# The end of a gated recurrence reordered, its states chained in place, and late weight tiles moved into its levels

## The chip, the cores and the metric

The kernel runs on one core of a Trainium2 chip. The metric is device time of one execution in microseconds (us); the table below gives the median of three runs. One more execution was profiled, and every row in this document that is marked as a profile comes from such a profiled execution.

## What is computed

Two layers of a diffusion backbone over 1024 latent tokens and 256 context tokens, model width 1024. Each layer mixes tokens with three groups of heads that read one input projection (A: neighbourhood attention, B: grouped attention with rotary positions, C: a gated recurrence that runs in both directions), joins them in one output projection, and then runs a gated convolutional feed-forward. Both halves are modulated by vectors computed from `c` and `c_ctx`, and each ends in a layer norm. What matters here:

```python
def gla_chunkwise(q, k, v, logf, s0):            # group C, chunks of 64 tokens
    def step(S, inp):
        qc, kc, vc, gc = inp
        b = jnp.cumsum(gc, axis=-2)
        ...
        att = jnp.einsum('bhtk,bhsk,bhtsk->bhts', qc, kc, decay)
        o = jnp.einsum('bhts,bhsv->bhtv', att, vc) + jnp.einsum('bhtk,bhkv->bhtv', qc * jnp.exp(b), S)
        b_last = b[..., -1:, :]
        S = S * jnp.exp(b_last[..., 0, :])[..., None] + jnp.einsum('bhsk,bhsv->bhkv', kc * jnp.exp(b_last - b), vc)
        return S, o

def hgrn2_readout(o, g, gn_g):
    y = rms_norm(o, gn_g) * jax.nn.silu(g)

# in each layer
mod = jnp.split((s_c @ w_ada[l] + b_ada[l])[:, None, :], N_MOD, axis=-1)     # w_ada[l]: 1024 x 6144
y = jnp.concatenate([o_a, o_b, o_c], axis=-1) @ w_out
x = layer_norm(DEEPNORM_ALPHA * x + mod[2] * y, ln1_g[l], ln1_b[l])
f = conv_ffn(modulate(x, mod[3], mod[4]), ...)                               # modulate(x) = layer_norm(x) * (1 + scale) + shift
```

The second layer gives out latent tokens only, so its projections run over 1024 columns where the first layer's run over 1280.

## The kernel before

The program of each engine is written out by hand; nothing is scheduled by a tool, and the order of a row in the source is the order on its engine. Engines wait for each other by semaphores. Activations lie by channel (128 channels x up to 1280 tokens, eight such tiles for width 1024). Every large product is made of three products of rounded halves: a weight tile is loaded (SyncE), split by GpSimd into a high and a low part (`split_tile`, L820 and on), an activation tile is split into `h_hi` (ScalarE, a copy) and `h_lo` (VectorE, a subtraction), and TensorE adds high by high, high by low and low by high (`gemm`, L1012). PSUM is used as two slots of three banks that take turns: a product may begin when the use before last of the slot has been read out ("freed"). `Plan` numbers these uses.

**Phase C, the recurrence.** Ten projections come first (forget gates f and b, input i, query q, gate g, each in two tiles of 128 channels, thus two heads each). Then the decay inside chunks of 64 is worked out by six levels (blocks of 1, 2, 4 ... 32): at each level and for each of the two tiles VectorE multiplies keys and queries in `c_x` by decays in `c_tot` (`longer`, L2075), ScalarE gathers keys into `c_ko`, TensorE makes the products within chunks (`att`, L1342 and L1346) and VectorE copies those that the level decides into `c_att` by a mask (`masked`, L2083). Behind the levels TensorE turns the keys (`turn_keys`, L872), ScalarE copies them to `c_kd`, TensorE makes what each chunk adds to its state (`added`, L1375) and ScalarE copies that to `c_d` (`take_added`). GpSimd spreads each chunk's whole decay over 64 values into `c_by` (`decays_by_value`, L840), and VectorE runs the states of all 20 chunks through one scan for each of four cases (two tiles, two directions; L2110) into `c_state`, which lies with the chunk as its last index, so that the 64 values of one chunk's state are 20 elements apart. `outputs` then adds for each tile the products with the own chunk (L1396) and with the incoming states (L1417), ScalarE takes the sum and its squares to `c_o`, TensorE averages the squares (`mean_squares`, L1428), ScalarE makes the reciprocal root and VectorE the gate (`gate`, L2125 and L2127).

**Late modulation tiles.** Of the modulation weights `w_ada`, 24 tiles of 1024 x 256 (1 MB) are not needed before a layer's end (16 in the second layer). In layer 0 eight of them are used during the projections; the other 16, and all 16 of layer 1, go through three slots of `ada_late`, which lie over the weight buffers that are idle during the levels. SyncE loads them (`load_late`), the first three when the last projection is done and each later one when the tile three before it has been used. TensorE uses them between the levels' products (`late`, L1038). Their sum is folded behind the outputs (L1048) and becomes `mods`.

**Phase O** is the output projection, whose first tile takes the eight activation tiles in `O_ORDER` as they become ready (0 to 2 from group A, 3 to 5 from B, 6 and 7 from C). ScalarE makes the first four high halves behind tile 0's reciprocal root (`end_of_recurrence`), VectorE the low halves behind tile 0's gate.

**Norm tails.** The layer norm behind phase O and behind the first feed-forward is not applied to the activations but folded into the next product by low rank rows. `norm_tail` runs three times: VectorE copies raw sums from PSUM to `sraw` (L1844), TensorE turns them so that tokens lie on partitions, VectorE works out mean and reciprocal deviation in some twenty steps on 12 values (`al`), writes three values per token into `colmat` in three parts (two alike, one negated), TensorE spreads first the reciprocal deviation and then `colmat` over a slot, and ScalarE and VectorE turn the latter into `rank_rows`: a rounded copy, and then the difference from it in the rows that `low_rows` marks (L1907). `correct` (L893) multiplies these rows.

## Time and profile before

| | us |
|---|---|
| median of three runs | 3658.02 |
| lowest and highest | 3657.78, 3658.77 |
| the profiled execution | 3653.44 |
| its span, first to last instruction | 3651.6 |
| TensorE products busy | 3436.2 (94%) |
| VectorE busy | 1634.5 (45%) |
| ScalarE busy | 1002.5 (27%) |
| GpSimd busy | 1077.7 (30%) |
| mean granted clock of TensorE | 0.979 |

Busy shares are means over phases that have different limits. Products overlap in the array, so a busy TensorE is not one at its peak. In the page and in the answers PE is TensorE, DVE is VectorE, ACT is ScalarE, POOL is GpSimd, SP is SyncE.

### The profile page before, as it was taken

What the parts mean: (1) busy time and instruction counts of PE and PEld (TensorE: products, weight loads), DVE (VectorE), ACT (ScalarE), POOL (GpSimd) and SP (SyncE); (2) the same over time, 40 slices, a digit from 0 to 9 for tenths busy, and PEclk for the clock granted to TensorE, in tenths of its full rate; (3) what the DMA queues carried; (4) which work ended last, traced back from release to release, by engine and by line L of the source; (5) the groups of instructions that cost most, each with busy time, mean ns of one, the idle gap of its engine ahead of it and who ended that gap; (6) DMA issues with size and microseconds to landing.
All of it is one profiled execution on the core that took longest, in us unless ns stands there. A gap on an engine that the chain in (4) does not pass through costs nothing.

```text
span 3651.6 us, 57048 instructions
## 1 busy us (share of the span) xinstructions
PE 3436.2 (94%) x24613; PEld 2836.9 (78%) x24613; DVE 1634.5 (45%) x2492; ACT 1002.5 (27%) x1435; POOL 1077.7 (30%) x408
## 2 busy tenths in 40 slices
PE   6999999979989999999999899999979899999998
PEld 5777778868868888888887677788867678888887
DVE  4333563065176334333434632463085563434436
ACT  4334564124122111111111333464133221111111
POOL 1212101304223333333332112201324244444443
PEclk9999999999989999999999899999989899999999
DMA  5111002252201111111112111001062111111111
GB/s 181 37 28 30 1 2 61 85 180 52 77 18 41 35 41 35 35 41 35 41 35 76 22 24 27 24 2 30 24 198 76 48 45 49 50 46 47 52 47 64
DMA packets 269677, 186.41 MB, mean 51 GB/s; under 512 B 45404, under 2 KB 249076, under 8 KB 269428
## 3 DMA queue, kind: packets, MB, share of 16 engines
q1 hardware_dynamic: 268272, 182.28, 16.7%
q8 instruction: 197, 3.23, 0.4%
q10 hardware_dynamic: 1156, 0.48, 0.1%
q14 instruction: 52, 0.43, 0.0%
HBM read 174.33 MB, written 8.39 MB: 50 GB/s over the span
## 4 chain that ended last, share of the span: by engine, by line
PE 84%; DVE 9%; issue 3%; ACT 2%; DMA 1%; POOL 1%; ACTq 0%; POOLq 0%; DVEq 0%; PEldq 0%
PE psum L1012 60%; PE psum L872 6%; PE psum L1112 5%; PE psum L881 3%; PE psum L1262 3%; PE psum L1190 2%; DVE f_t L2244 1%; DVE y_chan L2134 1%; DMA ada_late<-in_w_ada_dram 1%; PE psum L1417 1%; PE psum L941 1%; DVE c_x L2075 1%; PE psum L1221 1%; PE psum L1038 1%; ACT f_t L2774 1%
## 5 line engine op out<-in xcount | busy, mean ns | idle before, releaser
L1012 PE MATMUL psum<-h_hi,w_split 128*128 128x512 f32 (+1 forms) x5952 | 1438.0, 370 | 18.3 <-POOL w_split L834 8.1
L832 POOL TENSOR_SCALAR w_split<-w_raw 128x1024 fp32r<-128x1024 f32 x196 | 554.6, 2830 | 2308.3 <-PE psum L1012 1623.1
L1012 PEld LDWEIGHTS psum<-h_hi,w_split 128*128 128x128 f32 x5952 | 1030.7, 188 | 223.4 <-issue 12.1
L1012 PE MATMUL psum<-h_lo,w_split 128*128 128x512 f32 (+1 forms) x2976 | 800.1, 368 | 0.0
L1012 PEld LDWEIGHTS psum<-h_lo,w_split 128*128 128x128 f32 x2976 | 516.0, 188 | 97.6
L2244 DVE SCALAR_TENSOR_TENSOR f_t<-psum,vec,f_t 128x1023 f32<-128x1023 f32 (+1 forms) x264 | 260.2, 1013 | 704.5 <-ACT f_t L2774 701.3
L834 POOL TENSOR_TENSOR w_split<-w_raw,w_split 128x1024 fp32r<-128x1024 f32 x196 | 476.9, 2433 | 16.3
L1012 PE MATMUL psum<-f_hi,w_split 128*128 128x512 f32 (+1 forms) x1696 | 417.2, 371 | 15.7 <-DVE y_chan L2134 10.7
L2774 ACT ACTIVATE f_t<-psum,vec 128x1280 f32<-128x1280 f32 (+1 forms) x88 | 115.4, 1311 | 909.4 <-PE psum L1012 887.1
L1012 PEld LDWEIGHTS psum<-f_hi,w_split 128*128 128x128 f32 x1696 | 295.9, 188 | 80.4 <-issue 25.4
L2134 DVE SCALAR_TENSOR_TENSOR y_chan<-psum,mods,y_chan 128x1024 f32<-128x1024 f32 (+1 forms) x256 | 247.1, 1002 | 172.2 <-PE psum L1012 171.9
L1012 PE MATMUL psum<-f_lo,w_split 128*128 128x512 f32 (+1 forms) x848 | 233.8, 370 | 0.0
L1012 PEld LDWEIGHTS psum<-f_lo,w_split 128*128 128x128 f32 x848 | 149.3, 188 | 28.3
L872 PE MATMUL psum<-ident,o_chan 128*128 128x128 f32 x1016 | 151.6, 282 | 6.6 <-ACT a_pt L2348 3.1
L2436 ACT ACTIVATE o_chan<-o_chan,stats 128x1280 f32<-128x1280 f32 (+3 forms) x153 | 152.7, 998 | 0.0
L2348 ACT ACTIVATE b_pt<-psum 128x512 f32<-128x512 f32 (+1 forms) x204 | 113.5, 581 | 110.5 <-PE psum L872 110.5
L872 PEld LDWEIGHTS psum<-ident,o_chan 128*128 128x128 f32 x1016 | 108.2, 141 | 36.6 <-issue 28.2
L2050 DVE TENSOR_SCALAR c_tot<-c_x 128x2560 f32<-128x2560 f32 x4 | 6.0, 1490 | 288.4 <-PE psum L1012 288.4
L1112 PE MATMUL psum<-b_pt,b_v 128*64 128x128 f32 x1968 | 130.9, 278 | 0.4 <-DVE b_pt L1739 0.4
L1112 PEld LDWEIGHTS psum<-b_pt,b_v 128*64 128x64 f32 x1968 | 105.4, 137 | 18.1 <-issue 17.3
L1726 DVE CUSTOM_DVE_ANT_1 o_chan<-psum,zeros 128x1280 f32<-128x1280 f32 (+1 forms) x81 | 100.1, 1264 | 34.9 <-PE psum L1262 33.9
L2348 ACT ACTIVATE f_hi<-f_t 128x1280 fp32r<-128x1280 f32 (+1 forms) x44 | 51.4, 1168 | 194.0 <-DVE f_t L2257 194.0
(276 smaller groups left out, 3502.6 us busy)
## 6 DMA issues: line engine op xcount, KB each, us to landing
w_raw<-in_w_up_dram SPq DMA_DIRECT2D x88, 512.0 KB, 3.8
ada_late<-in_w_ada_dram SPq DMA_DIRECT2D x32, 1024.0 KB, 6.9
w_raw<-in_w_down_dram SPq DMA_DIRECT2D x44, 512.0 KB, 3.8
w_raw<-in_w_in_dram SPq DMA_DIRECT2D x42, 512.0 KB, 3.9
ada<-in_w_ada_dram SPq DMA_DIRECT2D x4, 2048.0 KB, 18.0
ada_early<-in_w_ada_dram SPq DMA_DIRECT2D x8, 1024.0 KB, 5.2
x_first<-in_x_dram SPq DMA_DIRECT2D x8, 512.0 KB, 12.7
o_x<-in_x_dram SPq DMA_DIRECT2D x8, 512.0 KB, 3.9
```

Source lines behind the costliest of these rows:

```text
L832: pool.tensor_scalar(w_hi[:, n % 2], w_raw[:, n % 2], 1.0, None, ALU.mult).then_inc(s["w_hi_done"], 1)
L834: pool.tensor_tensor(w_lo[:, n % 2], w_raw[:, n % 2], w_hi[:, n % 2].bitcast(F32), ALU.subtract)\
L872: return pe.transpose(out_ap, in_ap, ident[0:rows_, 0:rows_])
L881: last = pe.matmul(acc[:, t0:t0 + tn], weight, a[:, k, t0:t0 + tn], start=(k == 0 and j == 0), stop=(k == KT - 1 and j == 2))
L1012: last = pe.matmul(columns(key, t0, t0 + tn), weight, a[:, k, t0:t0 + tn], start=(k == order[0] and j == 0), stop=(k == order[-1] and j == 2))
L1112: last = pe.matmul(psum[rows_, OUT_BANK, 0:P], values(b)[:, rows_], turned_to(unit, head)[:, P * b:P * b + P], start=(k == 0), stop=(k == ...
L1262: ins = pe.matmul(scores_at(unit, hh)[:, t0:t0 + tn], q_[rows_], k_[rows_, t0:t0 + tn], start=pass_ == 0, stop=pass_ == 2)
L2134: ins = dve.scalar_tensor_tensor(out=y_chan[:, m, a:b], in0=columns(key, a, b), scalar=mods[:, l, KT * mod + m, who:who + 1], in1=base[:, ...
L2244: ins = dve.scalar_tensor_tensor(out=dst, in0=src, scalar=vec[:, at_col:at_col + 1], in1=dst, op0=ALU.mult, op1=ALU.add)
L2348: return act.activation(dst, src, ACT.Copy, scale=scale)
L2436: say(f"probs_ready{head}", act.activation(p, p, ACT.Exp, scale=-1.0, bias=stats[:, 0, c_:c_ + 1], accum_out=stats[:, 2, c_:c_ + 1]))
L2774: say("conv_start", act.activation(f_t[:, half, 0:w], slot(*key)[:, 0:w], ACT.Identity, scale=vec[:, mid:mid + 1], bias=vec[:, shift:shift ...
```

## The change

1. `c_state`, `c_by` and `c_d` go. ScalarE copies what chunks add straight into `c_x`, where the turned keys no longer are needed, chunk by chunk with 64 values side by side, and VectorE runs each state in place: 18 steps, for both directions in turn, each `state = state_before * decay + added` with the decay as a scalar per channel. `decays_by_value` on GpSimd goes.
2. `outputs` waits for the states behind the products with the own chunk, no longer ahead of them.
3. `O_ORDER` becomes 2, 3, 4, 5, 0, 1, 6, 7. The first four high halves stand ahead of ScalarE's `take_outputs(0)`, the first two low halves ahead of VectorE's new `mods`; `c_o` is moved so that they have room. Inside `outputs(1)` mean squares come behind four chunk pairs (two before) and the folding behind six (four before).
4. Late tiles: two are used behind level 0's products and none behind level 6's, where before it was none and three. The slots start from 0 in each layer, and the first three loads wait each for their own buffer only: the first for the last projection but one, the second for the last weight tile's split, the third for the last projection.
5. Norm tail: ScalarE copies the upper half of `sraw`. `colmat` is written by token as rounded values and their differences from the exact ones, so that `rank_rows` is one copy by ScalarE.

The diff, cut to its core:

```diff
-O_ORDER = [0, 1, 4, 5, 2, 3, 6, 7]
+O_ORDER = [2, 3, 4, 5, 0, 1, 6, 7]
...
-                sp.wait_ge(*full("C", l, C_PARTS[-1][0]))
+                first_free = [full("C", l, C_PARTS[-2][0]), (s["w_ready"], plan.tile["in", l, C_PARTS[-1][1]] + 1),
+                              full("C", l, C_PARTS[-1][0])]
                 for j in range(N_EARLY[l], len(late_tiles(l))):
+                    if j - N_EARLY[l] < 3:
+
+                        sp.wait_ge(*first_free[j - N_EARLY[l]])
                     load_late(j)
...
                 for n in range(len(STEPS) + 1):
                     for tile in range(2):
                         att(n, tile)
-                        if n:
-                            late(2 if n >= 3 and tile else 1)
+                        if n == 0:
+                            late(2 * tile)
+                        elif n < len(STEPS):
+                            late(2 if n > 1 and tile else 1)
...
-                for k, (tile, way) in enumerate(WAYS):
-                    dve.wait_ge(s["by_ready"], 4 * l + k + 1)
-                    dve.wait_ge(s["d_ready"], 4 * l + k + 1)
-                    say("state_ready", dve.tensor_tensor_scan(
-                        c_state[:, k].rearrange("p v i -> p (v i)"), c_by[:, k].rearrange("p v i -> p (v i)"),
-                        c_d[:, k % 2].rearrange("p v i -> p (v i)"), 0.0, ALU.mult, ALU.add))
+                for tile in range(2):
+                    passed = [None, None]
+                    for i in range(1, NCH - 1):
+                        for way in range(2):
+                            k = 2 * tile + way
+                            if i == 1:
+                                dve.wait_ge(s["d_ready"], 4 * l + k + 1)
+                            else:
+                                dve.wait_ge(*passed[way])
+                            ins = dve.scalar_tensor_tensor(out=state_of(k, i), in0=state_of(k, i - 1),
+                                                           scalar=c_el[:, tile, way, i:i + 1], in1=state_of(k, i),
+                                                           op0=ALU.mult, op1=ALU.add)
...
                 dve.wait_ge(s["late_used"], n_late(l))
                 take_modulation_rows(2 if l < DEPTH - 1 else 1)
+                for k in O_ORDER[0:2]:
+                    low_half(l, k)
                 dve.wait_ge(s["mods_full"], l + 2)
...
-                for p in (0, 2):
-                    w = P * groups_[p][1]
-                    last = also(dve.tensor_copy(sraw[32 * p:32 * p + 64, 0:w], psum[32 * p:32 * p + 64, 7, 0:w]))
+                say("sraw_ready", dve.tensor_copy(sraw[0:64, 0:P * groups_[0][1]], psum[0:64, 7, 0:P * groups_[0][1]]))
...
+                for part in (0, 4):
+                    also(dve.tensor_copy(to(part), four(high.bitcast(F32))))
+                last = also(dve.tensor_tensor(to(8), four(whole), four(high.bitcast(F32)), ALU.subtract))
...
-                dve.wait_ge(s["rank_hi"], st + 1)
-                dve.wait_ge(*release(dve.scalar_tensor_tensor(
-                    out=rank_rows[:, 0:w], in0=slot(*key)[:, 0:w], scalar=low_rows[:, 1:2], in1=rank_rows[:, 0:w].bitcast(F32),
-                    op0=ALU.mult, op1=ALU.add), *key))
```

How the order of instructions moves, at three places. In the lists `xN` counts equal instructions, and the brackets name the semaphores waited for. Line numbers behind the change are those of the changed kernel.

TensorE in layer 0, from the last of level 0's products to those of level 1 (`c_x 64x64` is level 0, `c_x,c_ko` level 1, `ada_late,cond` a late tile). Before:

```order
L1342 MATMUL psum<-c_x 64x64 [waits shared_bank]
L1342 MATMUL psum<-c_x 64x64 x7
L1346 MATMUL psum<-c_x,c_ko 64x64 [waits freed0,ko_ready,x_ready]
L1346 MATMUL psum<-c_x,c_ko 64x64 x35
L1346 MATMUL psum<-c_x,c_ko 64x64 [waits shared_bank]
L1346 MATMUL psum<-c_x,c_ko 64x64 x3
L1038 MATMUL psum<-ada_late,cond 32x128 [waits late_landed0]
L1038 MATMUL psum<-ada_late,cond 32x128 x15
```

And now:

```order
L1345 MATMUL psum<-c_x 64x64 [waits shared_bank]
L1345 MATMUL psum<-c_x 64x64 x7
L1041 MATMUL psum<-ada_late,cond 32x128 [waits late_landed0]
L1041 MATMUL psum<-ada_late,cond 32x128 x15
L1041 MATMUL psum<-ada_late,cond 32x128 [waits late_landed1]
L1041 MATMUL psum<-ada_late,cond 32x128 x15
L1349 MATMUL psum<-c_x,c_ko 64x64 [waits freed0,ko_ready,x_ready]
L1349 MATMUL psum<-c_x,c_ko 64x64 x35
L1349 MATMUL psum<-c_x,c_ko 64x64 [waits shared_bank]
L1349 MATMUL psum<-c_x,c_ko 64x64 x3
L1041 MATMUL psum<-ada_late,cond 32x128 [waits late_landed2]
```

Two late tiles have moved ahead of level 1's first products.

VectorE in layer 0, from the whole decays (`c_el`) to the gate of tile 0. Before:

```order
L2105 COPY c_el<-c_tot 128x2x19
L2110 SCALAR_TENSOR_TENSOR c_state<-c_by,c_d 128x1280 [waits dve_step,d_ready,by_ready]
L2110 SCALAR_TENSOR_TENSOR c_state<-c_by,c_d 128x1280 [waits d_ready,by_ready] x3
L1656 COPY mod_rows<-psum 128x256 [waits late_used]
L1661 TENSOR_TENSOR mods<-psum,vec 128x64 [waits dve_step,mods_full]
L1667 TENSOR_SCALAR mods<-mods 128x16 [waits dve_step]
L1661 TENSOR_TENSOR mods<-psum,vec 128x32 [waits dve_step]
L2125 SCALAR_TENSOR_TENSOR c_o<-c_o,head_g 128x1280 [waits dve_step,hg_rstd]
```

And now:

```order
L2101 COPY c_el<-c_tot 128x2x19
L2112 SCALAR_TENSOR_TENSOR c_x<-c_x,c_el 128x64 [waits dve_step,d_ready]
L2112 SCALAR_TENSOR_TENSOR c_x<-c_x,c_el 128x64 [waits d_ready]
L2112 SCALAR_TENSOR_TENSOR c_x<-c_x,c_el 128x64 [waits dve_step] x34
L2112 SCALAR_TENSOR_TENSOR c_x<-c_x,c_el 128x64 [waits d_ready] x2
L2112 SCALAR_TENSOR_TENSOR c_x<-c_x,c_el 128x64 [waits dve_step] x34
L1658 COPY mod_rows<-psum 128x256 [waits late_used]
L2132 TENSOR_TENSOR h_lo<-o_chan,h_hi 128x1280 [waits dve_step,o_hi_ready]
L2132 TENSOR_TENSOR h_lo<-o_chan,h_hi 128x1280 [waits o_hi_ready]
L1663 TENSOR_TENSOR mods<-psum,vec 128x64 [waits mods_full]
L1669 TENSOR_SCALAR mods<-mods 128x16 [waits dve_step]
```

Four scans have become 72 small steps, and two low halves stand ahead of `mods`.

ScalarE in layer 0, from the second copy of turned keys to the reciprocal root of tile 0. Before:

```order
L2348 ACTIVATE c_kd<-psum 128x1280 [waits full1]
L2348 ACTIVATE c_d<-psum 128x1280 [waits full0]
L2348 ACTIVATE c_kd<-psum 128x1280 [waits d_ready,full0,full1]
L2348 ACTIVATE c_d<-psum 128x1280 [waits state_ready,full0]
L2348 ACTIVATE c_d<-psum 128x1280 [waits d_ready,state_ready,full1]
L2348 ACTIVATE c_o<-psum 128x1280 [waits d_ready,full0]
L2673 ACTIVATE c_o<-psum 128x1280
L2681 ACTIVATE c_o<-psum 128x1280 [waits freed0,full0]
L2682 ACTIVATE c_o<-c_o 128x1280 [waits freed0]
L2348 ACTIVATE h_hi<-o_chan 128x1280 [waits hg_rstd]
```

And now:

```order
L2361 ACTIVATE c_kd<-psum 128x1280 [waits full1]
L2361 ACTIVATE c_x<-psum 128x2x10x64 [waits el_ready,full0]
L2361 ACTIVATE c_kd<-psum 128x1280 [waits d_ready,full0,full1]
L2361 ACTIVATE c_x<-psum 128x2x10x64 [waits full0]
L2361 ACTIVATE c_x<-psum 128x2x10x64 [waits d_ready,full1]
L2361 ACTIVATE h_hi<-o_chan 128x1280 [waits d_ready]
L2361 ACTIVATE h_hi<-o_chan 128x1280 x3
L2361 ACTIVATE c_o_156<-psum 128x1280 [waits full0]
L2689 ACTIVATE c_o_156<-psum 128x1280
L2697 ACTIVATE c_o_156<-psum 128x1280 [waits freed0,full0]
```

The copies of added products no longer wait for states, and four high halves stand ahead of the outputs.

## Rows read from the trace of the kernel before

**Rows 1.** The page, chain that ended last: share of the span by engine.

```profile
PE 84%; DVE 9%; issue 3%; ACT 2%; DMA 1%; POOL 1%; ACTq 0%; POOLq 0%; DVEq 0%; PEldq 0%
```

**Rows 2.** Time-line, VectorE, layer 0 levels: start, us, line, operation, count, [wait before].

```profile
766.65 1.49 DVE L2058 TENSOR_TENSOR c_x<-c_x,c_tot 128x1280 f32<-128x1280 f32 x1 [3.52 <-PE psum L1342]
...
811.05 2.89 DVE L2075 TENSOR_TENSOR c_x<-c_x,c_tot 128x1280 f32<-128x1280 f32 x2 [2.79 <-PE psum L1346]
...
824.35 2.89 DVE L2075 TENSOR_TENSOR c_x<-c_x,c_tot 128x1280 f32<-128x1280 f32 x2 [1.58 <-PE psum L1346]
```

**Rows 3.** The same of layer 1.

```profile
2662.62 1.49 DVE L2058 TENSOR_TENSOR c_x<-c_x,c_tot 128x1280 f32<-128x1280 f32 x1 [2.07 <-PE psum L1342]
...
2712.41 5.70 DVE L2075 TENSOR_TENSOR c_x<-c_x,c_tot 128x1280 f32<-128x1280 f32 x4 [2.28 <-PE psum L1346]
```

**Rows 4.** Time-line, TensorE, layer 0 levels.

```profile
764.28 2.01 PE L1342 MATMUL psum<-c_x 64*64 64x64 f32 x65 [4.58 <-issue]
...
803.42 1.08 PE L1038 MATMUL psum<-ada_late,cond 128*32 128x128 f32 x32 [1.24 <-DMA ada_late<-in_w_ada_dram]
```

**Rows 5.** Tile ada_late, its 32 loads of both layers.

```profile
DMA to landing us min/median/max: 5.0/6.9/11.6
```

**Rows 6.** Time-line, ScalarE, layer 0: last gather, turned keys, second added product.

```profile
824.35 2.85 ACT L2348 ACTIVATE c_att<-psum 32x640 f32<-32x640 f32 x4 [1.93 <-PE psum L1346]
828.30 2.37 ACT L2348 ACTIVATE c_kd<-psum 128x1280 f32<-128x1280 f32 x2 [1.10 <-PE psum L872]
...
834.91 1.24 ACT L2348 ACTIVATE c_d<-psum 128x1280 f32<-128x1280 f32 x1 [1.09 <-PE psum L1375]
```

**Rows 7.** Time-line, TensorE, end of layer 0's recurrence to its output projection.

```profile
837.49 2.14 PE L1375 MATMUL psum<-c_v,c_kd 64*64 64x64 f32 x120 [0.24 <-issue]
...
845.43 8.92 PE L1417 MATMUL psum<-c_x,c_state 64*64 64x64 f32 x146
...
858.12 2.42 PE L1428 MATMUL psum<-c_o,means 128*128 128x512 f32 x6
...
862.51 0.66 PE L1048 MATMUL psum<-fold,mod_rows 128*128 128x64 f32 x4
...
868.88 0.83 PE L1012 MATMUL psum<-h_hi,w_split 128*128 128x512 f32 x3 [0.32 <-DVE h_lo L2156]
```

**Rows 8.** Time-line, VectorE, layer 0: the scans, and a small product.

```profile
832.51 19.12 DVE L2110 TENSOR_TENSOR_SCAN c_state<-c_by,c_d 128x1280 f32<-128x1280 f32 x4 [4.55 <-ACT c_d L2348]
...
863.21 0.23 DVE L1661 TENSOR_TENSOR mods<-psum,vec 128x64 f32<-128x64 f32 x1 [11.26 <-PE psum L1048]
```

**Rows 9.** Time-line, GpSimd, layer 0: first split behind the first projection tile.

```profile
888.28 2.82 POOL L832 TENSOR_SCALAR w_split<-w_raw 128x1024 fp32r<-128x1024 f32 x1 [29.32 <-PE psum L1012]
```

**Rows 10.** Time-lines, layer 1: ScalarE's turned keys, projection's beginning, GpSimd's split.

```profile
2720.61 2.37 ACT L2348 ACTIVATE c_kd<-psum 128x1280 f32<-128x1280 f32 x2 [3.07 <-PE psum L872]
...
2757.48 0.70 PE L1012 MATMUL psum<-h_hi,w_split 128*128 128x512 f32 x2 [1.22 <-issue]
...
2772.71 2.88 POOL L832 TENSOR_SCALAR w_split<-w_raw 128x1024 fp32r<-128x1024 f32 x1 [22.89 <-PE psum L1012]
```

**Rows 11.** Time-lines, first norm tail: VectorE, TensorE, VectorE, TensorE.

```profile
1010.20 1.01 DVE L1844 COPY sraw<-psum 64x384 f32<-64x384 f32 x2 [3.00 <-PEq L653]
...
1017.09 2.39 PE L872 MATMUL psum<-ident,al 128*128 128x128 f32 x10 [5.16 <-DVEq L1887]
...
1022.55 1.55 DVE L1907 SCALAR_TENSOR_TENSOR rank_rows<-psum,low_rows,rank_rows 128x1280 fp32r<-128x1280 f32 x1 [0.27 <-ACT rank_rows L2348]
...
1024.16 1.21 PE L893 MATMUL psum<-rank_rows,wvec 12*128 12x512 f32 x2 [3.00 <-DVE rank_rows L1907]
```

**Rows 12.** Time-lines, GpSimd and VectorE, at the same time in phase O.

```profile
906.28 2.39 POOL L834 TENSOR_TENSOR w_split<-w_raw,w_split 128x1024 fp32r<-128x1024 f32 x1
...
906.62 2.08 DVE L1804 TENSOR_TENSOR ln_a<-ln_ch,mods 128x8 f32<-128x8 f32 x1
```

**Rows 13.** Windows, second tail: us, five engines' busy time, clock, DMA share, GB/s.

```profile
2000.00:2024.00 24.00, 12.94 (x38) 8.95 (x38) 18.29 (x41) 5.87 (x8) 0.00 (x0) 0.50 0.01 1
```

126 lines of the change are left out of this document (64 added, 62 removed).

## The prediction

> **What bounds the kernel now.** I read the chain of waits first: TensorE holds 84% of it, VectorE 9%, and nothing else more than 3% [rows 1]. The large products before and behind the recurrences run without a gap, so the change can only take time out of stretches in which TensorE waits or crawls. Then I read the time-lines of both recurrences, engine by engine, and of the three norm tails.
>
> In a recurrence's levels VectorE is the bound. Its rows stand back to back, and its only waits in layer 0 are 3.52, 2.79 and 1.58 us, each released by TensorE [rows 2], together 7.89; in layer 1 they are 2.07 and 2.28, together 4.35 [rows 3]. TensorE was late for two reasons. It stood 4.58 us in the first product with nothing waited for ("issue"), right after three late loads of 1 MB had been started at once, and later it waited for a late tile [rows 4]. A late load takes 5.0 to 11.6 us to land [rows 5].
>
> At the end of layer 0's recurrence ScalarE's first copy of turned keys begins at 828.30 [rows 6]; I call this T and count from it. TensorE is through the added products at T+11.3, waits for the first two scans (all four take 19.12 us [rows 8]), spends 8.92 us on 146 rows of state products, and starts the output projection at T+40.6 [rows 7]. (One small product of the program is two rows of the trace.)
>
> **The levels.** The first three late loads no longer start together behind the last projection. Two of them start one weight tile earlier, when nothing is loaded, and only 1 MB is in flight when the first products want their instructions. The stop of 4.58 us could be 1.06 us (less VectorE's 3.52) without VectorE noticing, and I take it that no more than that is left; if half of it stays, 1.2 us a layer are lost. Two late products now stand ahead of level 1: TensorE does them while VectorE builds its totals. From there each level wants three tiles in about 9 us, and each slot has a level between its use and its next one, against the 5 to 7 us of most landings. The last level has no late product left, so turning the keys follows it at once. Then VectorE's 7.89 us go and its last multiplication, with which ScalarE's second gather of 2.84 us starts [rows 2, 6], begins at 816.46. T moves from 828.30 to 819.3: **9.0 us**. In layer 1 the last four multiplications begin at 2712.41 less 4.35, 2708.06, two gathers of 2.4 us follow, and T is 2712.9 where it was 2720.61 [rows 3, 10]: **7.7 us**. TensorE's own waits for late tiles lay beside these and are not counted again.
>
> **The recurrence's end, layer 0.** GpSimd's spreading of decays and the four scans go. In their place VectorE gets 18 steps in two ways, 36 products of 64 elements a tile, each waiting for the one before it of its own way. The nearest row is one of 64 elements, 0.23 us [rows 8]. Two ways interleaved cost per pair between 0.23 us (each hides in the other) and 0.46 (nothing overlaps); I take 0.35, the middle, thus 6.3 us a tile. The second added product is copied by T+7.9 [rows 6], so the states are ready at T+14.2 and T+20.5. The Trainium skill (VectorE: DVE Perf Modes, section on the TRN2 errata) speaks against such a split: many small tiles each pay the fixed latency, and it advises 512 elements or more. With its fixed term of about 150 cycles one product here would be an estimated 0.22 us. The row agrees.
>
> State products read their weights with a step of 20 elements before and contiguously after. Before, 8.92 us for 146 rows are 61 ns a row; the added products, contiguous, take 2.14 us for 120, 17.8 ns [rows 7]. But these use four quarters of the array (chunk by head), and state products only two (head by head). The cost lies between 17.8 and 61 ns, and I take twice the first, 35.6: 5.4 us for the 152 rows of a tile. SBUF — State Buffer of the Trainium skill, in the box on cachelines of its section on the DMA port swizzle, says that a step is free up to 4 elements of fp32. The rows agree that 20 costs something.
>
> TensorE then: added products to T+11.3, own-chunk products of tile 0 to 12.9 (they no longer wait for states), a wait to 14.2, states to 19.6, own-chunk of tile 1 to 21.0, states 5.4, mean squares 2.4, folding 0.66 [rows 7]: 29.4 against 40.6, 11.2 us. VectorE (20.5) and ScalarE are just ahead of it: the four high halves that now precede the outputs are four copies of 1.2 us [rows 6] from T+12.7, through at 17.5, before tile 0's outputs at 19.6. VectorE's two low halves fit between its states and the folding. The projection's new order keeps the second gate in sixth place, so its wait of some 1.5 us stays. The end of the first projection tile, where GpSimd's wait ends at 888.28 [rows 9], follows its beginning: **11.3 us**.
>
> **Layer 1** has 128 state rows a tile (4.6 us). ScalarE's copy of the old mean stands between the end and the projection, 2.4 us in both kernels. By the same steps the projection begins at T+29.5 (before: T+36.9) and its first tile ends at T+43.9 (before: T+52.1) [rows 10]; I take **7.8 us** between the two.
>
> **The three norm tails.** The second evacuation of sums goes to ScalarE beside VectorE's (1.01 us for two, so about 0.43 saved). The low part of the rank rows is made by token while TensorE still spreads the first column, 2.4 us, which hides the 0.3 us that it costs more; were that cover gone, 0.3 us a tail. VectorE's 1.55 us over 1280 columns goes from the path to TensorE's wait of 3.00 us [rows 11]. That is 2.0, 2.0 and, for 1024 columns, 1.8 us: **5.8 us**.
>
> **Sum.** 9.0 + 7.7 + 11.3 + 7.8 + 5.8 = 41.6 us; 1.0 off for GpSimd (C, below) leaves 40.6. Against the profiled execution, 3653.44 us (span 3651.6 and 1.8 around it), that gives 3612.8. The median of the runs is 3658.02, so **3617.4 us**.
>
> **Rivals.** Within 0.2%, 7.3 us, is what a measurement of this kernel can hardly tell from no change.
>
> A, chance 0.12: state products gain nothing from contiguous weights, since their two quarters set the pace. 61 ns a row stays, tile 0 ends at T+23.5, the projection begins at T+37; 7.8 us are lost in layer 0 and 6.4 in layer 1: 3632. For it: two quarters are used in both kernels. Against it: 61 is 3.4 times 17.8, more than a halved array explains.
>
> B, 0.13: contiguous weights run at 17.8 ns and pairs at 0.3. Then VectorE's chain and ScalarE's halves lead, and 5 and 4 us more are gained: 3608.
>
> C, 0.09: GpSimd now splits the first two output tiles up to 25 us earlier, under VectorE's last level and in layer 1 perhaps under its states. A VectorE product of 8 elements took 2.08 us beside a 2.39 us GpSimd subtraction and ended with it [rows 12]. Four such holds a layer are 8.3 us, of which some 2 lie in slack: 12 us lost, 3629. My sum holds 0.5 a layer. SBUF — State Buffer of the Trainium skill says in its section on the two sides that GpSimd and a VectorE instruction with two SBUF inputs take a pair of ports as a lock for a whole instruction. The rows agree that the hold lasts until GpSimd's end.
>
> E, 0.06: late loads stay the pace of the levels, at 5 to 11.6 us each [rows 5]. Then the stop and the last level's products are saved and some 10 of the 16.7 us are not: 3627.
>
> D, slower, 0.04: the chained products are paced by their semaphores. From 0.93 us a pair on the states are 20.4 us behind TensorE in each layer and the whole gain is used up; at 1.2 the time is 3678. Around 0.93 nothing would be measured (0.03). Against it: 0.23 us for the like.
>
> The forecast has 0.53. So faster 0.93, same 0.03, slower 0.04. The granted clock adds a spread: 24 us behind a tail ran at 0.50 [rows 13], the 1.2 GHz level, after TensorE had waited through most of the tail; a shorter tail may move such a stretch by some us either way. The forecast's own range is 3609 to 3624. With B, C and E inside and A at its edge the range is **3604 to 3634**.
>
> **What would show it.** VectorE without waits above 0.5 us in the levels; TensorE waiting under 1 us in all for late tiles; T near 819 in layer 0 and, with 24.3 us gained ahead of it, near 2689 in layer 1; state steps at 0.35 us a pair; state rows at 36 ns; the projection at T+29; TensorE reading the rank rows straight behind ScalarE's copy. State steps above 0.5 a pair, holds beside GpSimd's splitting, or state rows near 60 ns would make it wrong.

## The result and the profile of the changed kernel

| | before | changed |
|---|---|---|
| median, us | 3658.39 (4 runs) | 3637.67 (4 runs) |
| lowest and highest | 3657.78, 3659.34 | 3634.21, 3639.89 |
| the profiled execution's span | 3651.6 | 3638.1 |

The ratio of the changed time to the time before is 0.9942, with a 95% interval of 0.9925 to 0.9959. The forecast was 3617.4 with a range of 3604 to 3634: the direction was right, half of the gain was not there. Measured again later (e9), the same kernel gave 0.9931 (0.9918 to 0.9944). One execution differs from the next by several us (3634.21 to 3639.89 here), so single traces are read for what waits for what, and the sums from medians. One execution of the kernel before, of the 27 beside e1 to e4, took 6699 us and is left out of the ratios. In the profiled execution the phases ahead of layer 0's recurrence, in which nothing was changed, took 5.6 us more than before, hence the later start of the rows below.

The chain that ended last has the same shares as in [rows 1], one point less of VectorE:

```profile
PE 84%; DVE 8%; issue 3%; ACT 2%; DMA 1%; POOL 1%; ACTq 0%; POOLq 0%; DVEq 0%; PEldq 0%
```

**Levels, layer 0.** The time-line of VectorE (columns as in [rows 2]) should have had no wait left. Eight are left, 7.1 us in all (7.89 before); the first and the last of them:

```profile
769.42 1.49 DVE L2054 TENSOR_TENSOR c_x<-c_x,c_tot 128x1280 f32<-128x1280 f32 x1 [0.66 <-PE psum L1345]
...
822.83 2.90 DVE L2071 TENSOR_TENSOR c_x<-c_x,c_tot 128x1280 f32<-128x1280 f32 x2 [2.34 <-PE psum L1349]
```

TensorE's waits over the levels (what it waited for, us in all, times, longest) tell why. Before:

```profile
PE psum L1346 <- DVE c_att L2083: 8.4, 5, 2.7
PE psum L1038 <- DMA ada_late<-in_w_ada_dram: 5.0, 3, 1.9
PE psum L1342 <- issue: 4.6, 1, 4.6
PE psum L1346 <- issue: 4.1, 4, 1.4
```

Changed:

```profile
PE psum L1349 <- issue: 12.3, 7, 3.5
PE psum L1345 <- issue: 2.6, 1, 2.6
PE psum L1041 <- DMA ada_late<-in_w_ada_dram: 1.8, 2, 1.5
```

The stop of 4.58 us in [rows 4] is down to 2.6 and the waits for late tiles to 1.8, but "issue" on the levels' products rose from 8.7 to 14.9 us (12.7 in e9, the same kernel), while the waits for VectorE fell from 8.4 to 1.7. The two together stayed at about 17 us: TensorE is as late as before, under another name. It was not that the loads of layer 0 became denser: over its levels DMA moved 222 GB/s, against 233 before. TensorE stops seven times inside the levels' products, and nothing is left for it to wait for but its own instructions. The trace's packet records bear this out: instructions have a DMA queue of their own, with packets of 16 KB (q8 on the page, 13 of them here), and each of TensorE's nine stops in these levels ends 2.2 to 2.7 us behind the start of such a packet. In the traces of all the other kernels here the stops put down to "issue" in both layers' levels do the same, within 2.2 to 3.3 us. In layer 1 the late tiles were the larger miss, 6.1 us where the prediction had under 1 (before: 3.5):

```profile
PE psum L1041 <- DMA ada_late<-in_w_ada_dram: 6.1, 5, 1.8
```

The clock and the busy time in two stretches (windows as in [rows 13]; the columns behind the length are TensorE, weight loads, VectorE, ScalarE, GpSimd) follow. The second row is layer 0's levels and shows the second limit: VectorE alone is busy 64.2 of 71.7 us.

```profile
848.20:855.00 6.80, 5.25 (x98) 5.28 (x100) 6.80 (x36) 2.08 (x2) 0.00 (x0) 0.50 0.01 2
761.00:832.70 71.70, 51.87 (x1803) 45.01 (x1802) 64.24 (x52) 26.20 (x25) 1.85 (x1) 0.86 0.69 222
```

**End, layer 0.** ScalarE, VectorE, TensorE, TensorE, where [rows 6 to 8] have the old rows. T is 832.67:

```profile
832.67 1.24 ACT L2361 ACTIVATE c_kd<-psum 128x1280 f32<-128x1280 f32 x1
...
836.82 1.26 DVE L2112 SCALAR_TENSOR_TENSOR c_x<-c_x,c_el 128x64 f32<-128x64 f32 x1 [2.45 <-ACT c_x L2361]
840.56 16.10 DVE L2112 SCALAR_TENSOR_TENSOR c_x<-c_x,c_el 128x64 f32<-128x64 f32 x71 [2.48 <-ACT c_x L2361]
...
849.75 6.84 PE L1420 MATMUL psum<-c_x 64*64 64x64 f32 x146 [2.80 <-DVE c_x L2112]
...
858.11 2.08 PE L1420 MATMUL psum<-c_x 64*64 64x64 f32 x64
...
866.30 0.82 PE L1015 MATMUL psum<-h_hi,w_split 128*128 128x512 f32 x3 [0.31 <-PE psum L1420]
```

The states are there at T+16.9 (the first tile's; TensorE starts on them at T+17.1) and T+24.0, forecast T+14.2 and T+20.5. The chain starts in time (its second way at T+7.9), but one step of it takes 2.39 us in place of 0.28, the largest of the 144 (line, count: ns min/median/max), beside a subtraction of GpSimd, which now splits the output tiles here:

```profile
L2112 DVE SCALAR_TENSOR_TENSOR c_x<-c_x,c_el x144: 272/276/2386, 836.8 to 2733.9; 128x64 f32<-128x64 f32 x144
```

```profile
840.82 2.43 POOL L846 TENSOR_TENSOR w_split<-w_raw,w_split 128x1024 fp32r<-128x1024 f32 x1
```

The state rows of tile 1 take 32.5 ns each (64 in 2.08 us), forecast 35.6; tile 0's take 47 ns, and the clock stood at 0.50, the 1.2 GHz level, through most of them (the first windows row above). The projection begins at T+33.6, forecast T+29.4, before T+40.6 [rows 7].

**End, layer 1.** VectorE, GpSimd, ScalarE, VectorE, TensorE twice (against [rows 10]); T is 2710.68:

```profile
2712.86 2.35 DVE L2101 COPY c_el<-c_tot 128x38 f32<-128x38 f32 x1
...
2712.78 2.39 POOL L846 TENSOR_TENSOR w_split<-w_raw,w_split 128x1024 fp32r<-128x1024 f32 x1
...
2715.36 1.24 ACT L2361 ACTIVATE c_x<-psum 128x1280 f32<-128x1280 f32 x1 [2.00 <-DVEq L2102]
...
2719.82 14.32 DVE L2112 SCALAR_TENSOR_TENSOR c_x<-c_x,c_el 128x64 f32<-128x64 f32 x71 [2.91 <-ACT c_x L2361]
...
2734.29 2.75 PE L1420 MATMUL psum<-c_x 64*64 64x64 f32 x64 [2.17 <-DVE c_x L2112]
...
2744.99 0.70 PE L1015 MATMUL psum<-h_hi,w_split 128*128 128x512 f32 x2 [1.23 <-issue]
```

A copy of 38 elements lasts as long as GpSimd's subtraction beside it, and ScalarE stands 2.00 us for it. The last states are there at T+23.5 (forecast T+20.5), and TensorE waits 2.17 us for them: in this layer VectorE's chain leads, which the prediction had just ahead of TensorE. The projection begins at T+34.3, forecast T+29.5, before T+36.9.

**First norm tail**, in the order of [rows 11]: VectorE and ScalarE copy the sums together, and TensorE reads the rank rows straight behind ScalarE's one copy; its wait of 3.00 us is 1.33.

```profile
1007.62 0.55 DVE L1844 COPY sraw<-psum 64x384 f32<-64x384 f32 x1 [3.00 <-PEq L661]
...
1007.61 0.38 ACT L2361 ACTIVATE sraw<-psum 64x256 f32<-64x256 f32 x1 [1.69 <-PEq L661]
...
1019.81 0.73 PE L895 MATMUL psum<-rank_rows,wvec 12*128 12x512 f32 x2 [1.33 <-ACT rank_rows L2361]
```

### The profile page after: what moved, and what is told of

It is laid out like the page before. It is cut to its first block, busy times and chain, and to the rows that moved or that the text cites. A ratio compares the mean times of both kernels' runs of the same rounds, so it can differ in the third digit from the quotient of the medians.

```text
span 3638.1 us, 57152 instructions
## 1 busy us (share of the span) xinstructions
PE 3429.5 (94%) x24613; PEld 2826.7 (78%) x24613; DVE 1629.4 (45%) x2613; ACT 1004.5 (28%) x1438; POOL 1040.0 (29%) x400
## 4 chain that ended last, share of the span: by engine, by line
PE 84%; DVE 8%; issue 3%; ACT 2%; DMA 1%; POOL 1%; ACTq 0%; POOLq 0%; DVEq 0%; PEldq 0%
PE psum L1015 60%; PE psum L874 7%; PE psum L1115 5%; PE psum L883 3%; PE psum L1265 3%; PE psum L1193 2%; DVE f_t L2257 1%; DMA ada_late<-in_w_ada_dram 1%; PE psum L1041 1%; DVE y_chan L2148 1%; PE psum L943 1%; PE psum L1224 1%; DVE c_x L2112 1%; ACT f_t L2792 1%; PE psum L1349 1%
## 5 line engine op out<-in xcount | busy, mean ns | idle before, releaser
L1115 PEld LDWEIGHTS psum<-b_pt,b_v 128*64 128x64 f32 x1968 | 105.3, 136 | 18.1 <-issue 17.3
```

Of the source, the lines that this page charges most:

```text
L1115: last = pe.matmul(psum[rows_, OUT_BANK, 0:P], values(b)[:, rows_], turned_to(unit, head)[:, P * b:P * b + P], start=(k == 0), stop=(k == ...
```

## The experiments

Three chips were used, one for e1 to e4, one for e5 to e8, one for e9 to e12; the kernel before has medians of 3657.94, 3657.41 and 3659.12 on them, and each ratio is to the kernel before on the same chip. This table is worked out from the time-lines of one execution each: us behind the last projection's last product, for T, for the decays (VectorE's copies to `c_el` all done), for all states, and for the output projection's first product. A single trace is good to some 2 us, in layer 1 to less: in the four kernels with the old levels (before, e2, e3, e6) T lies between 70.7 and 73.0 in layer 0 and between 67.7 and 71.9 in layer 1.

| kernel | layer 0: T, decays, states, projection | layer 1 | median, us | ratio |
|---|---|---|---|---|
| before | 72.9, 72.5, 96.2, 113.4 | 67.7, 65.9, 89.6, 104.6 | | |
| changed | 71.6, 73.3, 95.6, 105.2 | 63.4, 68.0, 86.9, 97.8 | 3637.67 | 0.9942 |
| e1 levels alone | 72.2, 72.9, 96.6, 113.9 | 66.4, 67.7, 91.3, 106.4 | 3657.94 | 0.9999 |
| e2 tails alone | 70.7, 71.0, 94.7, 112.0 | 68.7, 66.3, 90.2, 105.3 | 3651.96 | 0.9982 |
| e3 end alone | 72.7, 72.7, 98.6, 108.5 | 71.9, 67.4, 96.2, 106.0 | 3649.02 | 0.9978 |
| e4 quarter loads | 67.3, 73.5, 92.9, 101.2 | 62.3, 68.5, 87.2, 97.9 | 3626.24 | 0.9916 |
| e5 quarter products | 64.6, 69.2, 87.5, 96.3 | 60.5, 62.2, 84.9, 94.0 | 3623.22 | 0.9906 |
| e6 states side by side | 73.0, 73.0, 96.6, 109.3 | 68.0, 66.7, 90.4, 104.0 | 3655.77 | 0.9995 |
| e7 splits held | 73.2, 73.9, 95.9, 104.3 | 64.9, 66.4, 87.1, 97.8 | 3633.15 | 0.9931 |
| e8 four chains | 72.1, 73.7, 97.4, 113.0 | 65.3, 69.9, 92.6, 109.0 | 3654.9 | |
| e9 changed again | 71.8, 75.4, 95.3, 104.1 | 65.5, 70.0, 89.0, 98.8 | 3634.05 | 0.9931 |
| e10 levels and end | 70.1, 71.8, 93.8, 103.3 | 64.9, 69.4, 89.0, 98.2 | 3639.0 | 0.9948 |
| e11 half as many | 66.5, 70.9, 89.3, 98.1 | 63.0, 65.2, 86.2, 95.8 | 3624.99 | 0.9916 |
| e12 half and held | 66.3, 67.2, 87.4, 96.1 | 63.0, 64.5, 84.9, 96.0 | 3622.99 | 0.9906 |

### The parts one by one: e1, e2, e3, e10

e1 is part 4 of the change as the diff above shows it, e2 part 5, e3 parts 1 to 3; e10 is e1 and e3 together. The lines that mark them:

```diff
e1, e10:  -  sp.wait_ge(*full("C", l, C_PARTS[-1][0]))
          +  sp.wait_ge(*first_free[j - N_EARLY[l]])
          -  late(2 if n >= 3 and tile else 1)
          +  late(2 * tile)                       # behind level 0
          +  late(2 if n > 1 and tile else 1)     # behind levels 1 to 5
e2:       +  say("sraw_upper", copy(sraw[64:P, 0:many], psum[64:P, 7, 0:many]))
e3, e10:  -  dve.tensor_tensor_scan(c_state[:, k]..., c_by[:, k]..., c_d[:, k % 2]..., 0.0, ALU.mult, ALU.add)
          +  dve.scalar_tensor_tensor(out=state_of(k, i), in0=state_of(k, i - 1), ...)
```

> The kernel before with part 4 of the change alone (late tiles from level 0 on, first loads two tiles ahead); the whole reference is computed. Theory (TensorE in the levels is paced by its supply of instructions, which the moved products don't lessen): the wait for level 0's issue stop only moves into the later levels, the copy of turned keys in layer 0 comes some 1 to 2 us earlier and in layer 1 some 3 to 4 us earlier, and the time is 2 to 6 us below the kernel before. Rival one (the prediction as it stood, the changed kernel's levels were held by something else, such as clock): 16.7 us less, about 3642 us. Rival two (the moved loads collide): no gain or a loss.

Measured 3657.94, 0.9999 (0.999 to 1.0008): nothing. The expectation of 2 to 6 us failed as the 16.7 of the forecast did. The number is that of rival two, but not its reason: in layer 0 TensorE waits 0.5 us in all for late tiles, 5.0 before. T comes 0.7 and 1.3 us earlier, which is within the scatter, and the decays and the projection do not. In layer 1 GpSimd's spreading of the decays ran for 17.8 us from the moment VectorE was through with its last level. Before and in e1:

```profile
2718.97 17.79 POOL L840 TENSOR_SCALAR c_by<-c_el 128x1280 f32<-128x1280 f32 x4 [85.10 <-DVEq L2106]
```

```profile
2727.28 17.80 POOL L845 TENSOR_SCALAR c_by<-c_el 128x1280 f32<-128x1280 f32 x4 [86.82 <-DVEq L2110]
```

In the kernel before, VectorE's first scan in layer 1 waited 5.99 us for ScalarE's copy of what chunks add; in e1 it waits for GpSimd, and TensorE's wait for the scans grows from 2.2 us to 5.2 (waits, VectorE and TensorE, end of the recurrence):

```profile
DVE c_state L2114 <- POOL c_by L845: 3.6, 1, 3.6
PE psum L1401 <- DVE c_state L2114: 5.2, 1, 5.2
```

> The kernel before with part 5 alone (three norm tails: sums copied by two engines, low rank rows by token); the whole reference is computed. Theory: each of three tails is about 2 us shorter, as predicted, 5.8 us, and up to 2 us more where a stretch at half clock behind the tail becomes shorter: 6 to 8 us below the kernel before. Rival (the tails' gain in the trace was the clock's and would not stand by itself): under 4 us.

Measured 3651.96, 0.9982 (0.9974 to 0.9991): 6.0 us, as forecast (5.8).

> The kernel before with parts 1 to 3 alone (states chained in place, outputs before the states, output order); the whole reference is computed. Theory: the output projection begins some 33.6 us behind the first copy of turned keys in layer 0 (40.6 before) and 34.3 in layer 1 (36.9 before), with states ready 16 and 24 us behind that copy; 9 to 12 us below the kernel before. Rival (the prediction as it stood: states 14.2 and 20.5 us behind, projection 29.4): 18 to 19 us less. The three kernels e1 to e3 are to sum to the whole change (20.7 us) within 4 us if the parts don't help or hinder each other.

Measured 3649.02, 0.9978 (0.9969 to 0.9987): 8.9 us. Half of the forecast's 18.1 (it has 11.3 and 7.8, less 1.0), and just under the 9 to 12 expected. The three parts alone sum to 14.9 us, not to 20.7 or more. The trace of layer 1 shows what e3 lacks. TensorE's time-line at the end of the levels in e3:

```profile
2717.58 1.08 PE L1034 MATMUL psum<-ada_late,cond 128*32 128x128 f32 x32 [0.34 <-DMA ada_late<-in_w_ada_dram]
2720.81 0.85 PE L1034 MATMUL psum<-ada_late,cond 128*32 128x128 f32 x21 [2.14 <-DMA ada_late<-in_w_ada_dram]
2722.65 1.07 PE L1034 MATMUL psum<-ada_late,cond 128*32 128x128 f32 x11 [1.00 <-issue]
2723.65 4.53 PE L868 MATMUL psum<-ident,c_x 128*128 128x128 f32 x20
```

The late tiles that still stand behind the last level hold up the turning of keys (L868), and VectorE, decays ready, waits 9.67 us for what the chunks add:

```profile
2731.22 2.17 DVE L2112 SCALAR_TENSOR_TENSOR c_x<-c_x,c_el 128x64 f32<-128x64 f32 x1 [9.67 <-ACT c_x L2361]
```

> The kernel before with parts 1 to 4 of the change, all but the norm tails; the whole reference is computed. Part 4 alone gave nothing and parts 1 to 3 alone 8.9 us. Theory (the parts need each other: behind the levels of the kernel before GpSimd's spreading of the decays set the end, and it starts with VectorE's last level and not with TensorE's, so an earlier end of TensorE's levels was worth nothing; once the spreading is gone, what chunks add sets the start of the state chain, and that comes behind TensorE's last late product): together they give 13 to 16 us, about 3643. Rival (they simply add, and the rest of the whole was scatter): 8 to 10 us, about 3648.5.

Measured 3639.0, 0.9948 (0.9935 to 0.9961): 20.1 us, more than the theory's 13 to 16 and far above the rival's 8 to 10. In its trace the turning follows the level's products, with a wait for VectorE only:

```profile
2703.30 3.46 PE L1347 MATMUL psum<-c_x,c_ko 64*64 64x64 f32 x128
2708.35 1.28 PE L873 MATMUL psum<-ident,c_x 128*128 128x128 f32 x10 [1.58 <-DVE c_x L2075]
```

So part 4 is worth nothing alone and 11 us (by the medians on two chips) once parts 1 to 3 are in; the intervals of e3 and e10 don't meet. That it is the spreading, out of parts 1 to 3, that makes the difference is what the waits of e1 point to; no run takes it away by itself.

> The changed kernel itself, beside the next three on one chip, so that they can be compared with it. It gave a ratio of 0.9942 with an interval of 0.9925 to 0.9959 to the kernel before; I expect 0.994 again, some 3637 us, within 2 us.

Measured 3634.05, 0.9931, 3 us below the expected 3637; the interval, 0.9918 to 0.9944, holds both. It is 5.0 us below e10 on the same chip: the tails again.

### What holds the levels: e4, e5, e11

```diff
e4:  -  sp.dma_start(home, w_ada[m]...[:, :, a:a + ADA_LATE_W])
     +  few = KT if j < N_EARLY[l] + 3 else KT // 4
     +  sp.dma_start(home[:, 0:few], w_ada[m]...[:, 0:few, a:a + ADA_LATE_W])
e5:  -  for k in range(KT // 2):            # of each late tile in the levels
     +  for k in range(1):
e11: -  for k in range(KT // 2):
     -      for part in range(4):
     -          upper, half = divmod(part, 2)
     -          matmul(psum[32 * part:32 * part + 32, 7, P * group:P * group + P],
     -                 cond[:, KT // 2 * upper + k, ...], weight(KT // 2 * upper + k)[:, P * half:P * half + P])
     +  for k in range(KT // 4):
     +      for part in range(4):
     +          matmul(psum[32 * part:32 * part + 32, 7, 2 * P * group:2 * P * group + 2 * P],
     +                 cond[:, KT // 4 * part + k, ...], weight(KT // 4 * part + k))
```

> The changed kernel in which each late weight tile behind the first three of a layer brings only its first quarter of rows (the rest of the buffer keeps what it held, so the modulations are not the reference's); all instructions stay. Theory (TensorE's instruction chunks of 16 KB come over the same DMA engines as the loads and wait behind them): with a quarter of the traffic a chunk is there about 3.5 us after the one before it is used up and not 5 to 6, the idle time put down to issue in layer 0's levels falls from about 15 us to under 6, no wait for late loads is left, and both layers' levels are 6 to 10 us shorter each: 10 to 18 us below the changed kernel, about 3622. Rival one (instruction supply is slow by itself): issue waits stay above 12 us and only the 2 us of waits for loads go: 1 to 4 us less. Rival two (VectorE's level chain paces, issue gaps only fill its waits): TensorE's waits turn into waits for VectorE, and the time changes by under 4 us.

Measured 3626.24, 0.9916 (0.9902 to 0.993), against 0.9942 and 0.9931 of the changed kernel: 5 to 10 us less. TensorE's waits in layer 0's levels:

```profile
PE psum L1350 <- DVE c_att L2080: 14.9, 8, 2.9
PE psum L1346 <- issue: 2.8, 1, 2.8
```

With a quarter of the traffic the same instructions arrive in time: 14.9 us of "issue" become 2.8. This shows the cause of the stops. But the time does not follow by as much: 14.9 us of waits for VectorE stand in their place, T comes 4.3 and 1.1 us earlier, and the decays not at all (against e9 by 1.9 and 1.5). Part of this is the experiment's own doing. The output weights landed sooner, so GpSimd split them under VectorE's last level, and VectorE's last four multiplications took 9.41 us where the changed kernel's took 5.68. VectorE and GpSimd in e4, then VectorE in the changed kernel, layer 0:

```profile
820.08 9.41 DVE L2072 TENSOR_TENSOR c_x<-c_x,c_tot 128x1280 f32<-128x1280 f32 x4
822.75 3.15 POOL L847 TENSOR_TENSOR w_split<-w_raw,w_split 128x1024 fp32r<-128x1024 f32 x1
...
827.25 5.68 DVE L2071 TENSOR_TENSOR c_x<-c_x,c_tot 128x1280 f32<-128x1280 f32 x4
```

With a held copy of decays (2.33 us in place of 0.18) that is 5.9 us of holds in each layer. The changed kernel has some 3 us of such holds a layer, so the 5 to 10 us may understate what the full traffic costs. The waits went as the second rival says, the time went further than its 4 us and not as far as the theory.

> The changed kernel in which TensorE makes only the first four of the sixteen products of each late tile inside the levels (the modulations are not the reference's); all loads stay. It leaves out 192 products with their weight loads in each layer, three of the 14 instruction chunks of layer 0's levels. Theory (the levels are held by instruction chunks that queue behind loads, with VectorE's chain of the levels close behind): loads now follow each other faster and still crowd the chunks, the levels of layer 0 are 3 to 5 us shorter, those of layer 1 1 to 3 us, the decays leave VectorE no more than 2 us earlier: 3 to 9 us below the changed kernel. Rival (TensorE's own work in the levels paces them): 16 us of busy time gone in each layer would give 15 us or more in all.

Measured 3623.22, 0.9906 (0.9892 to 0.9919): 9 to 13 us below the changed kernel, above the expected 3 to 9 and below the rival's 15. The decays come 4.1 and 5.8 us earlier, where at most 2 was expected. In layer 1 the levels' mean granted clock was 0.61 (0.83 in e9), so this gain was had although much of that stretch ran at the 1.2 GHz level. VectorE and late loads share the rest:

```profile
PE psum L1349 <- DVE c_att L2079: 9.2, 7, 2.9
PE psum L1040 <- DMA ada_late<-in_w_ada_dram: 4.4, 2, 3.6
PE psum L1040 <- issue: 3.8, 1, 3.8
```

> The changed kernel with every modulation product made over 256 columns in place of 128, four quarters of the sum in the four row groups of PSUM in place of two halves of sum by two halves of columns; so half as many products with the same columns through the array, and the whole reference is computed. Tells instruction supply from array time, both of which e5 lessened: e5 left out 192 products a layer, three chunks of instructions and 16 us of busy time, and was 13 us faster. This one leaves out 128 products in each layer's levels, two chunks, and no columns. Theory (chunks queueing behind loads are what counts, some 3.5 to 5 us each while they are not hidden, VectorE's chain close behind): 4 to 8 us below the changed kernel. Rival one (array time counted): within 1.5 us of it. Rival two: a product of 256 columns holds its row group longer and the late tiles take more time, a loss.

Measured 3624.99, 0.9916 (0.99 to 0.9931), 9.1 us below the changed kernel on the same chip (3634.05) by the medians and 5.5 by the ratios; four of its five executions are below all five of e9. Groups of TensorE by line over layer 0's levels (busy us, mean ns | idle before), first the changed kernel (e9), then e11:

```profile
L1041 PE MATMUL psum<-ada_late,cond 128*32 128x128 f32 x512 | 23.4, 351 | 0.6 <-DMA ada_late<-in_w_ada_dram 0.6
L1349 PE MATMUL psum<-c_x,c_ko 64*64 64x64 f32 x960 | 22.7, 241 | 13.2 <-issue 9.9 <-DVE c_att L2079 3.3
```

```profile
L1352 PE MATMUL psum<-c_x,c_ko 64*64 64x64 f32 x960 | 20.7, 238 | 6.4 <-issue 3.2 <-DVE c_att L2085 3.2
L1041 PE MATMUL psum<-ada_late,cond 128*32 128x256 f32 x256 | 20.3, 431 | 7.3 <-DMA ada_late<-in_w_ada_dram 4.3 <-issue 3.1
```

The same columns went through the array in half as many instructions. The busy time of the late tiles falls by 3.1 us and "issue" on these two lines from 9.9 to 6.3, but waits for late tiles rise from 0.6 to 4.3, so the idle time as a whole stays (13.8 and 13.7). The levels' own products, the same in both, are 2.0 us shorter: e11's layer 0 had a mean clock of 0.92 over the levels, e9's 0.83. Layer 1 has nearly one clock in both (0.84 and 0.83), and there "issue" falls from 11.0 to 6.5 us and T comes 2.5 us earlier. So the number of their instructions, not their columns, is a large part of what the late tiles cost, and the first rival (within 1.5 us) falls; in layer 0 the clock has a share that no run separates. By the table 6.0 us of the gain arise in layer 0 and 3.0 in layer 1. How they divide between fewer instructions to bring and fewer to issue stays open.

### The recurrence's end: e6, e7, e8, e12

```diff
e6 (on the kernel before):
-  c_state[rows_, 2 * tile + way, :, i - 1],
+  c_state[rows_, 2 * tile + way].rearrange("p v i -> p (v i)")[:, HD * i - HD:HD * i],
e7 and, on e11, e12 (GpSimd, ahead of the output tiles' splits):
+  pool.wait_ge(s["state_ready"], 4 * l + 4)
e8: the loop over i outside, over all four k inside
```

> The kernel before in which the products with incoming states read 64 neighbouring values of the state buffer as their weights, in place of 64 that lie 80 bytes apart (other values, so the outputs of the recurrence are not the reference's); nothing else differs. Theory (the step of the weights is what costs): a product with a state takes 33 ns per row of the trace and not 61, so tile 0's 146 rows take 4.9 us and not 8.9. The first tile's products come while the last states are still being made, so at most the second tile's 4 us count in each layer: 4 to 8 us below the kernel before. Rival (the pace comes from the half clock or from the two-quarter shape, not the step): 61 ns stay and the time stays within 1 us.

Measured 3655.77, 0.9995 (0.9986 to 1.0005): at most 5 us less, and it can't be told from nothing. That the rows become shorter is shown; TensorE's time-line of layer 0:

```profile
847.99 6.27 PE L1417 MATMUL psum<-c_x,c_state 64*64 64x64 f32 x152
...
866.64 0.81 PE L1012 MATMUL psum<-h_hi,w_split 128*128 128x512 f32 x3 [3.06 <-DVE h_lo L2156]
```

41 ns a row in place of 61 [rows 7], though the clock stood at the 1.2 GHz level for more than half of these 6.27 us, and 32 rows of tile 1 in 1.15 us, 36 ns. 3 us of what it frees become a wait for VectorE's low halves; the projection is 4.2 us earlier in layer 0 and 0.6 in layer 1. Why the median shows less than these 4.8 us is open. The clock may be part of it: its mean over the ten runs is 0.9760, over the 15 of the kernel before 0.9773, and among the 26 runs beside e1 to e4 0.001 less went with 1.5 us more, loosely.

> The changed kernel in which GpSimd splits the first two output weight tiles only when all states are made, in place of as soon as they have landed; the whole reference is computed. Theory (GpSimd's splits beside them hold VectorE's last short steps of the levels and the first state steps): the copies of the decays take 0.2 us each and not up to 2.35, the decays are ready some 1.5 us earlier in layer 0 and 2.5 in layer 1, and the output projection begins 1 to 3 us earlier in each layer: 2 to 5 us below the changed kernel. Rival one (the start of the state chain is set by what chunks add, which comes later than the decays anyway): within 1 us. Rival two (splits come too late for the first output tile): 7.1 us of splits behind the last state end some 2 us ahead of the projection, so a loss only if the states come over 2 us sooner.

Measured 3633.15, 0.9931 (0.9918 to 0.9943). Against the changed kernel's 0.9942 it is 4 us, against e9's 0.9931 nothing. VectorE's time-line of layer 1 shows the holds gone, the copy at 0.17 and every step equal:

```profile
2707.05 0.17 DVE L2105 COPY c_el<-c_tot 128x38 f32<-128x38 f32 x1
...
2713.87 14.00 DVE L2116 SCALAR_TENSOR_TENSOR c_x<-c_x,c_el 128x64 f32<-128x64 f32 x71 [2.76 <-ACT c_x L2365]
```

The decays come 1.6 us earlier in layer 1, and the chain waits for what the chunks add. From T on, the states come 1.3 us earlier in both layers (T+22.7 and T+22.2, from T+24.0 and T+23.5), but T itself was later in this trace. The hold is removed as the theory says; its worth lies between rival one's nothing and 4 us.

> The changed kernel in which VectorE takes the four state chains in turn (72 steps, four apart) in place of two and two; the whole reference is computed. Tells latency from occupancy: if a step of 0.23 us in layer 0 and 0.20 in layer 1 is the wait for the step before it in its own chain, four in turn overlap and take under 0.15 us each; if it is what each instruction costs VectorE, they stay at 0.20 to 0.23. I expect the latter. The first tile's states are then ready only with the last ones, so the output projection begins some 3 to 6 us later in each layer and the time is 6 to 12 us above the changed kernel.

Measured 3654.9 in one run, 17 to 21 us above the changed kernel, not 6 to 12: the projection comes 8 and 11 us later than in the changed kernel, not 3 to 6. VectorE and TensorE in layer 1:

```profile
2730.36 13.60 DVE L2112 SCALAR_TENSOR_TENSOR c_x<-c_x,c_el 128x64 f32<-128x64 f32 x69 [1.07 <-ACT c_x L2361]
...
2743.71 6.49 PE L1420 MATMUL psum<-c_x 64*64 64x64 f32 x125 [11.91 <-DVE c_x L2112]
```

0.197 us a step with four chains, 0.197 with two (14.00 us for 71, above): so it is what each instruction costs VectorE, not a wait for the step before it. TensorE waits 11.91 us here, and 1.57 us in the changed kernel, where the chains go tile by tile. Behind the long wait its rows took 52 ns each, at a mean clock of 0.55, which adds to the loss.

> e11 with GpSimd's splits of the output tiles held until the states are made, as in e7; the whole reference is computed. e7 was 4 us below the changed kernel by medians of two different chips, while its trace showed only 1 us of that at the recurrences' ends. If e7's hold is worth 1 us, this is within 2 us of e11; if it is worth 4, it is 3 to 5 below e11. I expect 1 to 2 us below e11 and 5 to 10 us below the changed kernel.

Measured 3622.99, 0.9906 (0.989 to 0.9921): 2.0 us below e11, which may be nothing, and 11 us below the changed kernel on the same chip, just over the 5 to 10 expected. T lies 6.5 and 4.7 us ahead of that of the kernel before: this is how much of the forecast's 9.0 and 7.7 for the levels was reached at last, with half as many instructions for the late tiles. With e11 it is the fastest kernel here that computes the whole reference.

## Why the prediction was half right

By its terms, in the traces of the changed kernel and of e9:

- **Levels, 9.0 and 7.7 us: this step failed.** T moved by 1.1 to 1.3 us in layer 0 and 2.2 to 4.3 in layer 1, and part 4 alone gave nothing (e1). What was wrong is the claim that TensorE would no longer be late once the first three loads were spaced and the late tiles moved. That took the stop of 4.58 us for the cost of three loads started together. It is a standing cost: the same number of instructions has to come, in packets, beside the loads, and "issue" was 14.9 us in place of 8.7, while the waits for VectorE fell by as much (e4: 2.8 of "issue" with a quarter of the traffic). So most of VectorE's 7.89 us of waits stayed, 7.1. The sign was there: in the waits of the kernel before, shown above, the same "issue" stood four more times inside the levels' products, 4.1 us, and the sum has no term for it. In layer 1 the late tiles took 6.1 us and not under 1.
- **End, 11.3 and 7.8 us**: 7.0 to 8.3 and 2.6 to 3.6. The mechanism was right, the length of the state chain was mis-sized. A pair of steps is 0.39 us, inside its bounds but above the 0.35 taken: 0.8 us a tile. In layer 0 one step was held 2.1 us by GpSimd (e9: the chain's second way began 1.6 us late instead), in layer 1 the second way began at T+9.1 and not T+7.9 behind the held copy of decays; the sum had 0.5 a layer for this. In layer 1 these make the states 3.0 us late, and the projection with them. The state rows were right at the full clock (31 to 33 ns, forecast 35.6), but stretches at the 1.2 GHz level fell on them: layer 0's first tile lost 1.4 us in 6.8 us of it, and in layer 1 3.4 us of it, from 2735.8 on, cost some 1.7 us.
- **What the steps replaced.** Of the 19.12 us of scans [rows 8], the third took 5.54 us beside GpSimd's spreading and the last, with the spreading over, 3.58. Four of 3.58 are 14.3 us, as long as the 72 steps (14.2 at 0.197). By this estimate part 1's gain on VectorE came from GpSimd's spreading being gone, not from steps being cheaper than scans; no run tests it.
- **Tails, 5.8 us**: 6.0 alone (e2), 5.0 in the pair e9 and e10. With the projections of both layers 15.0 and 15.2 us earlier in the two traces this makes some 21 us, and the medians say 20.7.
- **The sum treated the parts as free of each other.** That did not hurt the sum for the whole, since all are in it, but it hid what carries what. T was taken as the clock of the end; in e1 that clock was GpSimd's spreading behind the decays, and in e3's layer 1 the late tiles that still stood behind the last level. Hence, as far as the traces tell, 0 and 8.9 us alone and 20.1 together.

Of the rivals, A (61 ns a row stay) is ruled out by 32.5 and by e6. B needed 17.8 ns: no. C (holds beside GpSimd) exists, 2.35 us for a copy of 0.18: some 3 us a layer in the traces of the changed kernel, up to 5.9 in e4, where it had 8.3 and the sum 0.5. Taking the holds away was worth at most 4 us in all and perhaps nothing (e7, e12), not the 12 that C has. E, with a chance of 0.06, is the nearest: loads pace the levels, though mainly through the instructions beside them; late tiles themselves held TensorE for long only in layer 1. It gave 3627 and took the end at full size. D fell with 0.39 us a pair. The rule of the Trainium skill weighed for the small steps (VectorE: DVE Perf Modes, section on the TRN2 errata) gave an estimate of 0.22 us a product; the runs say 0.197, also where nothing depends on the step before it.

## What to carry to other kernels

"Issue" on an engine with many small instructions is a cost that grows with their number and with the traffic beside them: merging two products into one of twice the columns gained 5 to 9 us here where moving the same products about gained nothing by itself. Before a step is credited with an earlier time of one engine, follow each of the other engines' chains to the same point: part 4 gained 0 or 11 us depending on whether parts 1 to 3 stood behind it. And a stretch in which one engine is busy 64 of 72 us holds at most 8 us, whatever waits its neighbours show, unless that engine's own work gets shorter.

## What the runs showed of the hardware

Instructions for TensorE come later beside loads: the same TensorE program had 14.9 us (e9: 12.7) of "issue" in layer 0's levels beside full loads and 2.8 beside a quarter of them, and each such stop ended 2.2 to 3.3 us behind the start of a 16 KB packet of instructions. Sixteen products of 128 columns a tile, and eight of 256, each in four row groups, took 23.4 and 20.3 us of busy time for the 16 late tiles in layer 0's levels, at mean clocks of 0.83 and 0.92. VectorE multiplications of two SBUF tiles of 1280 took up to 3.64 us beside GpSimd's splits (e4) and 1.48 without, a copy of 38 elements 2.35 and 0.18. A VectorE step of 64 elements with a scalar per channel costs 0.197 us whether two or four chains take turns. Products of 64 by 64 whose weights lie 80 bytes apart took 61 ns a row of the trace, side by side 31 to 36, and 41 to 53 where the 1.2 GHz level fell on them.
